# PEER gates: one-hot tables in the split format, made token by token, with the softmax weight as a high and a low half

## What is computed

```
q   = tokens @ wq                          # 8 heads, two halves of 128 each
s1  = q_half_1 . keys_1 ; s2 = q_half_2 . keys_2      # 128 keys a side
top 16 of each side, the 256 pair sums, and of these the top 16
w   = softmax(the 16 sums)                 # per head, so 8 x 16 = 128 picks a token
out = sum over picks of  w * gelu(token . u[i, j]) * v[i, j]      # expert (i, j), i and j in 0..127
```

## Time and profile before

| | us |
|---|---|
| timed runs | 4532.34, 4529.9, 4537.26 |
| median | 4532.34 |
| profiled execution | 4540.71 |
| its span | 4538.6 |

### The profile page before, as it was taken

How to read it: one execution, slowest core, us unless ns; L and a number is a source line. 1 busy time by engine, 2 the same in 40 slices (tenths; PEclk the granted TensorE clock), 3 DMA queues, 4 the chain that set the end, 5 groups by cost and what they waited for, 6 DMA issues and landing times. The chain is left out here.

```text
span 4538.6 us, 81488 instructions
## 1 busy us (share of the span) xinstructions
PE 4181.9 (92%) x30346; PEld 3823.7 (84%) x30346; DVE 3076.9 (68%) x5261; ACT 1815.6 (40%) x2655; POOL 37.9 (1%) x54
## 2 busy tenths in 40 slices
PE   8977999969888589999999899999988889999998
PEld 8956999849884489899888898998877589899887
DVE  5566565556523648887888588878872559887887
ACT  4324343334322434444333444443332444444333
POOL 0000000000000001000000010000000001000000
PEclk9988999979999899999999999999999999999999
DMA  6633666517430037655777475567752157556775
GB/s 231 208 128 101 228 202 225 175 53 234 151 114 19 19 121 216 187 175 178 235 234 235 148 229 175 176 193 234 234 184 77 36 154 229 174 175 193 235 236 184
DMA packets 300374, 786.59 MB, mean 173 GB/s; under 512 B 32848, under 2 KB 132176, under 8 KB 299344
## 3 DMA queue, kind: packets, MB, share of 16 engines
q1 hardware_dynamic: 300112, 782.95, 55.0%
HBM read 731.44 MB, written 51.38 MB: 172 GB/s over the span
## 5 line engine op out<-in xcount | busy, mean ns | idle before, releaser
L248 ACT ACTIVATE ring_hi<-ring 128x1024 fp32r<-128x1024 f32 x1166 | 1235.8, 1061 | 1929.2 <-PE banks L269 1239.6
L254 DVE TENSOR_TENSOR ring_lo<-ring,ring_hi 128x1024 fp32r<-128x1024 f32 x1166 | 1427.8, 1225 | 729.1 <-ACT ring_hi L248 715.7
L265 PE MATMUL banks<-h_parts,ring_hi 128*128 128x256 f32 x4848 | 1228.4, 291 | 106.1 <-ACT ring_hi L248 104.8
L266 PE MATMUL banks<-h_parts,ring_hi 128*128 128x256 f32 x4848 | 1205.3, 285 | 0.0
L265 PEld LDWEIGHTS banks<-h_parts,ring_hi 128*128 128x128 f32 x4848 | 942.1, 194 | 120.4 <-ACT ring_hi L248 59.4
L266 PEld LDWEIGHTS banks<-h_parts,ring_hi 128*128 128x128 f32 x4848 | 943.6, 195 | 0.3
L280 PE MATMUL banks<-h_parts,ring_hi 128*128 128x512 f32 x3048 | 763.5, 392 | 0.7 <-DVE h_parts L1676 0.7
L269 PE MATMUL banks<-h_parts,ring_lo 128*128 128x256 f32 x4848 | 685.7, 284 | 0.8 <-DVE ring_lo L254 0.6
L269 PEld LDWEIGHTS banks<-h_parts,ring_lo 128*128 128x128 f32 x4848 | 630.8, 194 | 2.5 <-DVE ring_lo L254 2.5
L280 PEld LDWEIGHTS banks<-h_parts,ring_hi 128*128 128x128 f32 x3048 | 548.2, 189 | 99.8 <-issue 1.8
L283 PEld LDWEIGHTS banks<-h_parts,ring_lo 128*128 128x128 f32 x3048 | 415.8, 190 | 29.7
(11 more groups left out here) (213 smaller groups left out, 3806.1 us busy)
## 6 DMA issues: line engine op xcount, KB each, us to landing
ring<-peer_u_dram SPq DMA_DIRECT2D x384, 512.0 KB, 3.9
ring<-peer_v_dram SPq DMA_DIRECT2D x384, 512.0 KB, 3.7
act_store<-acts_out SPq DMA_DIRECT2D x384, 128.0 KB, 3.2
scratch<-act_store SPq DMA_DIRECT2D x384, 128.0 KB, 3.5
ring<-ffn_gate_dram SPq DMA_DIRECT2D x88, 512.0 KB, 3.7
ring<-ffn_up_dram SPq DMA_DIRECT2D x88, 512.0 KB, 3.6
ring<-ffn_down_dram SPq DMA_DIRECT2D x88, 512.0 KB, 3.7
big<-mod_w_dram SPq DMA_DIRECT2D x80, 512.0 KB, 4.6
```

The source lines that it names most:

```text
L248: self.nc.scalar.activation(self.hi[:, n % 2], self.ring[:, self.slot(j)], ACT.Copy).then_inc(self.count("tile_hi").sem, 1)
L254: self.nc.vector.tensor_tensor(self.lo[:, self.slot(j)], self.ring[:, self.slot(j)], self.hi[:, n % 2].bitcast(F32), ALU.subtract).then_in ...
L265: self.nc.tensor.matmul(out, w, b_hi, start=opens and m == 0, stop=False)
L266: self.nc.tensor.matmul(out, w, b_lo, start=False, stop=False)
```

## The change

The two tables become F32R tables, and a product over them single-pass. A one is exact in F32R; the weight is not, so it is kept as a rounded high half and a rest, and each token gets two products that add up in the bank: A with the high table, A with the rest table. A step still handles four tokens, but as two halves of two tokens.

- ScalarE's copy of the weights rounds them (F32R); VectorE takes the rest once a stage, from the banks, into `lam`.
- `mark(n, half)` makes three tables for each of two tokens by tensor_scalar with per-partition scalars: (column number == first key), (column number == second key) x high weight, the same x rest. That is 12 operations of 128 columns a step in place of L1660 and L1663. The two buffers now alternate by half step; mark(n, half) waits for the products of (n-1, half).
- On VectorE mark(n, 0) stands ahead of the split and mark(n, 1) behind it.
- On TensorE gates(n, 0) stands between the high-part and the low-part products of the rise, gates(n, 1) behind the rise.

```diff
+        at_scratch = -(-nc.sbuf_base // 32) * 32
         self.scratch = sb("scratch", [P, 2048])
+        self.marks = nc.alloc_sbuf_tensor_at("marks", [P, 2, 3, 2, NKEYS], F32R, offset=at_scratch)
...
-    def three(self, pe, j, turns, terms, opens, n=None):
+    def three(self, pe, j, turns, terms, opens, n=None, between=None):
...
             self.nc.tensor.matmul(out, w, b_lo, start=False, stop=False)
+        if between is not None:
+            between()
         pe.wait_ge(lo.sem, turns * RING + lo.after(n + 1))
...
-            def gates(n):
-
-                pe.wait_ge(marks_weighted.sem, marks_weighted.after(n + 1))
+            def gates(n, half):
+
+                pe.wait_ge(marks_weighted.sem, marks_weighted.after(2 * n + half + 1))
                 pe.wait_ge(kept.sem, kept.after(n + 1 - R))
-                for t in range(B):
-                    last = nc.tensor.matmul(k.ps[:, n % R, t * P:(t + 1) * P], marks[:, n % 2, 0, t], marks[:, n % 2, 1, t],
-                                            start=True, stop=True)
+                for t in range(HALF):
+                    place = (half * HALF + t) * P
+                    for side in (1, 2):
+                        last = nc.tensor.matmul(k.ps[:, n % R, place:place + P], marks[:, half, 0, t], marks[:, half, side, t],
+                                                start=side == 1, stop=side == 2)
                 last.then_inc(product.sem, 1)
...
-                rise(e)
-                if 0 <= e - NS - GATES_LAG < STEPS:
-                    gates(e - NS - GATES_LAG)
+                n = e - NS - GATES_LAG
+                if 0 <= n < STEPS:
+                    rise(e, lambda: gates(n, 0))
+                    gates(n, 1)
+                else:
+                    rise(e)
...
-            def mark(n):
-
-                dve.wait_ge(product.sem, product.after(n - 1))
-                at = slice(n * B, (n + 1) * B)
-                nc.vector.tensor_tensor(marks[:, n % 2], iota, k.picks[:, 0:2, at].unsqueeze(3).to_broadcast([P, 2, B, NKEYS]),
-                                        ALU.is_equal).then_inc(marked.sem, 1)
-                dve.wait_ge(marked.sem, marked.after(n + 1))
-                nc.vector.tensor_tensor(marks[:, n % 2, 1], marks[:, n % 2, 1],
-                                        k.picks[:, 2, at].unsqueeze(2).to_broadcast([P, B, NKEYS]),
-                                        ALU.mult).then_inc(marks_weighted.sem, 1)
+            def mark(n, half):
+
+                dve.wait_ge(product.sem, product.after(2 * n + half - 1))
+                for t in range(HALF):
+                    at = n * B + half * HALF + t
+                    key, other_key = k.picks[:, 0, at:at + 1], k.picks[:, 1, at:at + 1]
+                    nc.vector.tensor_scalar(marks[:, half, 0, t], k.c("iota"), key, None, ALU.is_equal)
+                    nc.vector.tensor_scalar(marks[:, half, 1, t], k.c("iota"), other_key, k.picks[:, 2, at:at + 1],
+                                            ALU.is_equal, ALU.mult)
+                    last = nc.vector.tensor_scalar(marks[:, half, 2, t], k.c("iota"), other_key, weight_rest[:, at:at + 1],
+                                                   ALU.is_equal, ALU.mult)
+                last.then_inc(marks_weighted.sem, 1)
...
             dve.wait_ge(picked.sem, picked.after(3))
+            nc.vector.tensor_tensor(weight_rest, k.ps[:, 7, 0:T], k.picks[:, 2], ALU.subtract).then_inc(rest.sem, 1)
+            dve.wait_ge(rest.sem, rest.after(1))
             for n in range(N - NS):
                 if n < STEPS:
-                    mark(n)
+                    mark(n, 0)
                 if tile < N:
                     split()
+                if n < STEPS:
+                    mark(n, 1)
...
-                        nc.scalar.activation(k.picks[:, w], k.ps[:, 6 + w // 2, w % 2 * T:w % 2 * T + T],
-                                             ACT.Copy).then_inc(picked.sem, 1)
+                        place = k.picks[:, w] if w < 2 else k.picks[:, w].bitcast(F32R)
+                        nc.scalar.activation(place, k.ps[:, 6 + w // 2, w % 2 * T:w % 2 * T + T], ACT.Copy).then_inc(picked.sem, 1)
```

24 lines of the change are left out of this document (13 added, 11 removed).

## The result

The changed kernel takes 4574.49 us (median of 6 runs, 4571.34 to 4576.81) against 4532.83 for the kernel before beside it (6 runs, 4529.9 to 4537.26). The ratio is 1.0091, with a 95% interval of 1.0078 to 1.0104: slower by 0.9%. Its profiled execution took 4576.81 us with a span of 4574.7, which is 36.1 more than the span before.

The account below looks back on a forecast made before the run. TensorE bounds the kernel before at 3.767 us a step; afterwards VectorE's 3.96 does, losing 0.197 x 60 x 3 = 36 us, from median 4532.3 to 4568. Forecast's own range 4555 to 4590; with rival 1, 4531 to 4592.

Parts of the forecast that it names:

- The bound and the spare time: Gated stage before the change: TensorE sets the 3.767 us step; VectorE issues 3.01 us, about 0.76 to spare.
- TensorE's 0.114 a product: Gate products: each single-pass product is paced by its weight load at 0.114 us, eight 0.91, TensorE step 3.79.
- L792's loads: Nearest row for the product price: two-column products with full 128 x 128 weights, eight loads in 0.91 us, 0.114 each.
- the columns-only 0.065: Lower bound of a 128-column gate product if only columns counted: 0.065 us, TensorE step 3.40.
- +4 us alone: Halved passes on TensorE by themselves: (3.79 - 3.767) x 192 = 4 us slower.
- Pointer 0.061, operations of 0.194 and 0.255, cycle 3.96: VectorE's tables: each per-partition scalar costs 0.061 us; one-pointer operations 0.194, two-pointer 0.255; with the split's 1.14, cycle 3.96.
- The first rival, free pointers: VectorE's pointers cost nothing, cycle 3.4, TensorE keeps the bound: +3 to +14 us, 4535 to 4546, chance 0.17.
- turning point of 0.221 a mean operation: VectorE's tables: from 0.221 us a mean operation downwards the free-pointer case holds; expected 0.235, a thin margin.
- Who waits: TensorE waits at the second half's products for mark(n, 1), about 0.2 us a step; VectorE has no gap.
- mark(n+1, 0) has 1 us of slack: On VectorE, the first half's products of step n end 1 us before mark(n+1, 0) asks for them.
- 60 of 64 steps pay, 36 us: After VectorE's lead is used up, about 60 steps in each of three stages lose 0.197 us: 36 us.
- rivals 2 and 4: Narrow VectorE operations at plain rate plus pointers, 4715, chance 0.04; products not single-pass, +170 us, 0.03 including the unnamed.

Follow-up runs that it names:

- the run that has it alone: Changed kernel without each token's third table, the high half multiplied twice instead: 4536.95 us, 1.0006 of before.
- the run with constants: Changed kernel with constants in place of all per-partition scalars of the twelve table operations: 4532.92 us, a single run, against 4533.55 before.
- two runs in which the slack is gone: Changed kernel with mark(n, 1) ahead of the split: 4647.33 us; changed kernel with both halves' products behind the rise: 4644.84 us.
- The three misses: Changed kernel with wide tensor_tensor tables, 4612.41 us; with mark(n, 1) ahead of the split, 4647.33; with one 256-column product a token and tables shared among engines, 4552.06.
- the wide form: Changed kernel with a half step's tables made by three wide tensor_tensor operations without per-partition scalars: 4612.41 us, 1.0178.
- the first run with one load a token: Changed kernel with one 256-column product a token, ScalarE making rest tables, VectorE adding halves, GpSimd making every second first table: 4552.06 us, 1.0042.

## Why the prediction was right, step by step

- **The bound and the spare time.** TensorE set the pace and VectorE had some 0.7 us to spare. Shown by the run with half the products and two tables (3.32, 4452) and by the 0.72 of waiting that comes back with one table less.
- **TensorE's 0.114 a product, "halving the passes gives TensorE nothing".** Right in mechanism, a little high: 0.110 in two runs (0.88 for eight, 0.44 for four). L792's loads were the right row, the columns-only 0.065 is refuted. TensorE's step is 3.76, not 3.79, so the "+4 us alone" is not there; the time of the run that has it alone, 1.0006 (0.9997 to 1.0016), could not tell 4 us from none. The Trainium skill, TensorE: Matmul & The Clock Gate, gave two answers. Its section on LDWEIGHTS (107 ns for 128 columns) agrees with the measured 0.110; its section on the back-to-back issue gap (56, or about 81 ns sustained) does not hold for these operands.
- **Pointer 0.061, operations of 0.194 and 0.255, cycle 3.96.** Measured 0.197, 0.257 and 3.97. The durations came out at 269 and 330 ns for the 0.28 and 0.34 told beforehand. The price was built from L1689, MAX8 and L1362, none of which is such an operation, and the run with constants confirms it part by part (0.136 for the 0.133 taken). The rule of the Trainium skill in VectorE: DVE Perf Modes, section on the errata, gives 127 ns for the bare operation, near the 136 seen from start to start, and has no term for a pointer; by an estimate from it the cycle would be 2.66 and not the 3.97 measured. One bound of mine did not add up: with 0.068 a pointer, twenty pointers make the cycle 3.96 + 0.14 = 4.10 and the loss some 59 us, not 4.05 and 51. The measured 0.061 made it harmless.
- **The first rival, free pointers (0.17).** Refuted by the same run. Its turning point of 0.221 a mean operation held: the change has 0.236 (2.83 / 12) and is slower, the run with constants 0.136 and is not.
- **Who waits.** The second half's products for the marking, in 170 of 192 steps. The bracket shows 0.16, the starts 0.21; told were 0.2. VectorE without a gap, as told.
- **mark(n+1, 0) has 1 us of slack.** It is 0.8: the first half's products end at 1994.06 and the marking comes to them at 1994.89. What it is worth was underrated: two runs in which the slack is gone cost 70 to 73 us more than the change.
- **60 of 64 steps pay, 36 us.** 60 steps of each stage pay, as told, 0.206 each in the place of 0.197: 37 us, and 38.6 with the ends of the stages.
- **From span to time.** That the spans differ by 36.1, the forecast's 36 almost to the digit, is luck: the stages are 38.6 us longer, and the profile of before happened to be 2.5 us longer in the rest. The median lies 6.5 us above the forecast, for two reasons. The stages cost 2 to 3 us more than told. And the working had a small fault: I took the 8 us by which the profiled execution of before lay above the median off the profiled time of after as well, which lay only 2 above its own median. The medians differ by 41.7 us with 35 to 47 in the interval, which holds the 38.6, so the runs ask for no further mechanism.
- **The chances.** By their own list those for "slower" come to about 0.86 (0.72, half of 0.17, and rivals 2 and 4), not 0.81. Nothing hangs on it.
- **L1721, the weight's rest.** It takes 0.42 us as told, and the wait for L250 behind it is 2.74 as it was 2.75: hidden.

My expectations of the experiments were worse than the prediction. The three misses are of one kind: I added start-to-start times where one operation waits for another, within VectorE in the wide form, and in the other two round a chain that crosses engines, without following the loops that the new order closed.

## To carry to other kernels

Where a product with a small moving operand is priced by its weight load, as the products of up to 256 columns were here, saving passes gains nothing unless it saves loads: put operands that share a weight side by side in one product. Before work moves to the second engine, add up that engine's own cycle with the price of each per-partition scalar, and compare it with the idle time that its row shows per step. Then follow every loop of waits through the engines with full durations where one engine waits for another, since a loop can be longer than the sum of any engine.

## What was not expected of the hardware

- A wait of VectorE for its own previous operation costs 0.11 to 0.12 us over the unwaited handover: 0.72 against 0.61 for 512 columns, 0.46 against 0.34 for 256.
- A product in the split format costs TensorE 0.110 us at 128 columns, 0.12 at 256 (two in 0.24) and 0.230 at 512: up to 256 columns the width is almost free.
- An fp32 product of 128 columns takes two records of loads and so 0.22 us, the same as two split-format products of high and rest. That is why the change's TensorE side came out even to 0.01 us.
- GpSimd needs 799 ns for a table of 128 columns that takes VectorE 269, and VectorE's operations beside it last 353 and 369 ns instead of 330. The mean is over operations with and without an overlap. In the first run with one load a token the same operation on GpSimd lasts 1.93 and 0.60 us by turns. GpSimd's records are rough, and what the two engines share was not looked into.
